# Heads' output gates, squares, roots and scaling computed inside the token mixers, one head late

## The chip, the cores and the metric

One core of a Trainium2 chip runs the whole program. The metric is the device time of one execution in microseconds; before the change it was 4261.61 us, the median of 3 runs (4261.18 to 4262.74). Engines are called by their names: TensorE (PE for its matmuls, PEld for its weight loads), VectorE (DVE), ScalarE (ACT), GpSimd (POOL) and SyncE (SP), which issues most of the transfers.

## The reference

The program is one inference step of a small trunk of two layers over 640 tokens (128 context, 512 latent), model width 1024. Layer 0 mixes tokens with HGRN2, layer 1 with GLA; both are followed by a PEER expert mixer. What matters here is the end of each token mixer:

```python
def _gated_head_norm(o, gate, w):
    of = o.astype(f32)
    y = of * lax.rsqrt(jnp.mean(of * of, axis=-1, keepdims=True) + EPS)
    return y * w.astype(f32) * jax.nn.silu(gate.astype(f32))

def _hgrn2_mixer(h, w_in, lb, gnorm_w, w_out, s_f, s_b):
    z = h @ w_in            # q, iv, f_f, f_b, og
    ...
    o = _gated_head_norm(o, og.reshape(b_, L, H_A, DV_A), gnorm_w)
    return o.reshape(b_, L, DVT_A).astype(h.dtype) @ w_out, S_f, S_b
```

HGRN2 has 8 heads of value width 128, GLA 4 heads of value width 256. The normalisation is per token and head. Its output goes through the 1024 x 1024 matrix w_out, is scaled and added to the residual stream.

## The kernel before, in words

Activations lie transposed: 128 channels on the partitions, the 640 tokens along the row (T = 640, NT = 5 tiles of 128 tokens, DC = 8 chunks of channels, NV = 1 or 2 value chunks a head). fp32 products are made of three fp32r products of high and low parts, so every weight chunk is first split: w_hi by ScalarE, w_lo by VectorE or GpSimd.

`mixer` (L502) is one stage with one instruction stream per engine, and a loop over the heads in each stream. The first H - 1 heads run in a hardware loop, the last is written out with `final=True`. The order inside a head is written by hand.

- TensorE (`head` in the tensor block): `project` for the late chunks j (values, output gates og) and the first early chunk or two of the next head; transposes of keys and values (`turn`, L1158); scores into pS (`level_scores`, L1173, and `near_scores`, L1183); the state products (L1214); the rest of the next head's early chunks; the output products (L1227).
- ScalarE: `value_chunk` or `copy` takes projections out of the two banks pp (L787); `next_hi` splits weights (L768); `keep` stores doubled products (L849); `output_gates` copies og out; at the end of a head `decays(h + 1)` does the next head's sigmoids (L825 to L835), and then the head's output goes to oT tile by tile (L933).
- VectorE: the decayed queries (L1024), seven `double` steps (L1030, L1033) with a weight split `lo` between some of them (L1012), masks (L1076 to L1084), states (L1097). In GLA also the convolutions (L993).
- GpSimd: only a weight split for the next head (L738).
- SyncE: loads weights and states and stores each head's og to the memory buffer og_spill (L708).

`mix_out` (L1242) is the next stage. It loads og of all heads back (L1280), takes sigmoids on ScalarE (L1322) and products with og on GpSimd (L1303). ScalarE and VectorE square all of oT (L1318, L1411), TensorE sums the squares with one-column matmuls (L1348), VectorE makes the mean's inverse (L1417, L1419), ScalarE its root (L1324), TensorE spreads it over the partitions (`spread`, L1355). Per chunk k VectorE multiplies by the norm weight and gate (`gated`, L1395) and by the root (`normal`, L1403), ScalarE takes the high part (L1329), VectorE the low part (L1408), and TensorE multiplies with the first two output weight chunks (L1362). The other six weight chunks follow (w_hi L1315, w_lo L1298). A stage ends with a barrier over all engines (L55).

Of the kernel before, what the change touches and what calls it, by code (L numbers as in the profile page):

```python
# [16 lines left out]
P = 128  # L17
# [79 lines left out]
def build_program(nc, a, out, upto=99):  # L97

    x_sp = nc.dram_tensor("xT_spill", [P, DC, T], F32, kind="Internal").ap()
    og_sp = nc.dram_tensor("og_spill", [DC, P, T], F32, kind="Internal").ap()  # L100
# [3 lines left out]
    with ctx:  # L104
        c = {}
        for name, shape, dt in [
            ("ident", [P, P], F32), ("ones_d", [P, P], F32), ("ones_h", [P, P], F32),
            ("coarse_mask", [P, NT, P], BF16), ("fine_mask", [P, NF, FINE], BF16), ("room", [P, 624], F32),
# [52 lines left out]
def setup(nc, a, c, x_sp, x_saved):  # L161
# [4 lines left out]
    with ExitStack() as s:  # L166
# [49 lines left out]
        def _(pool):  # L216
# [6 lines left out]
            pool.memset(c["one"][:, :], 1.0)  # L223
            pool.memset(fold[:, :], 0.0)
# [277 lines left out]
def mixer(nc, a, c, mx, h_hi, h_lo, og_sp, out, layer, x_saved):  # L502
# [7 lines left out]
    s_new = out[3 if mx.gla else 2][0, 0]  # L510
    L, E = len(mx.late), len(mx.early)
# [11 lines left out]
    with ExitStack() as s:  # L523
# [3 lines left out]
        w_raw = [sb(f"w_raw{i}", [P, DC, P]) for i in range(2)]  # L527
        w_hi = [sb(f"w_hi{i}", [P, DC, P], F32R) for i in range(2)]
        w_lo = [sb(f"w_lo{i}", [P, DC, P], F32R) for i in range(2)]
# [21 lines left out]
         o_done, o_out, s_in, s_out, og_done, og_out, q_sig_done, sp_passed, act_passed) = (  # L551
            sem(n) for n in ("w_hi_done", "lo_first", "lo_dve", "proj", "copied", "f_ready", "qk_ready", "turned",
                             "turned_out", "kv", "s_done", "att", "masked", "o_done", "o_out", "s_in", "s_out",
                             "og_done", "og_out", "q_sig_done", "sp_passed", "act_passed"))
# [8 lines left out]
        block = s.enter_context(nc.Block())  # L563

# [24 lines left out]
        def chunks_done(h, j):  # L589

            return h * NCH + (PRE + E + made(j) + 1)

# [86 lines left out]
        def _(sp):  # L679
# [12 lines left out]
            def head(h, final):  # L692
# [25 lines left out]
            sp.sem_inc(og_out, 16)  # L718
# [12 lines left out]
            sp.wait_ge(og_out, 16 * H + 16)  # L731

        @block.gpsimd
        def _(pool):
# [6 lines left out]
            def head(h, final):  # L741
                if not final:
# [14 lines left out]
            with pool.Fori(0, H - 1) as h:  # L757
                head(h, False)
# [3 lines left out]
        def _(act):  # L762
# [101 lines left out]
            def output_gates(h, n, final, which=BOTH):  # L864
                if n == 0 and 0 in which:
                    act.wait_ge(og_out, h * 16 + 16)
                copy(og[:, n, :], NV + n, h, which=which)
                if 1 in which:
                    next_hi(h, NV + n, final)

            def head(h, final):

                if mx.gla:
# [25 lines left out]
                    act.drain().then_inc(og_done, 1)  # L899
# [11 lines left out]
                else:  # L911
# [6 lines left out]
                    act.drain().then_inc(og_done, 1)  # L918
                    keep(h, 3, 5)
                    if not final:  # L920
                        early(h, 0, (0,))
                    keep(h, 5, 7)
# [8 lines left out]
                for t in range(NT):  # L931
# [3 lines left out]
                    if t == 2 and mx.gla and not final:  # L935
                        decay_exp(h + 1)

# [23 lines left out]
            with act.Fori(0, H - 1) as h:  # L961
# [4 lines left out]
        def _(dve):  # L966
# [48 lines left out]
            def head(h, final):  # L1015
# [9 lines left out]

                def double(s0, s1):
# [11 lines left out]
                if mx.gla:  # L1038
# [18 lines left out]
                else:  # L1057
# [9 lines left out]
                    lo(h, 2, final)  # L1067
                    double(1, 3)
                    lo(h, 3, final)
                    double(3, 7)  # L1070
                    lo(h, 4, final)

                dve.wait_ge(att, h + 1)
# [14 lines left out]
                for i, (d, t) in enumerate(WITH_STATE):  # L1088
# [10 lines left out]
                    dve.drain().then_inc(s_done, 1)  # L1099
# [1315 lines left out]
```

## Time and profile before

| | us |
|---|---|
| median of the runs | 4261.61 |
| the profiled execution's own time | 4259.91 |
| its span, first to last instruction | 4258.0 |
| TensorE matmuls busy | 3923.1 (92%) |
| VectorE busy | 3443.8 (81%) |
| ScalarE busy | 1704.9 (40%) |
| GpSimd busy | 1835.2 (43%) |
| mean granted TensorE clock | 0.954 |

The HGRN2 mixer and its output projection lie between about 99 and 635 us of the span, those of GLA between about 2257 and 2675 us. The rest is setup, retrieval and the expert mixers, which the diff does not touch. A timeline row reads: start, duration, engine, line, operation, output<-inputs, shape, count of merged instructions, and in brackets the idle time before it with what released it. A fp32 matmul of the plain type counts as two instructions (x2). Neighbouring matmuls overlap, so their price is the distance of their starts, not their duration.

### The profile page before, as it was taken

To read this page: it belongs to the slowest core of one execution; us is meant where nothing else is said; L and a number is where in the kernel's file an instruction comes from. 1 tells how busy PE (TensorE), PEld (TensorE's weight loads), DVE (VectorE), ACT (ScalarE), POOL (GpSimd) and SP (SyncE) were. 2 spreads that over 40 slices of the span, in tenths; PEclk is the share of its full clock that TensorE was granted. 3 is DMA by queue.
4 is the path that set the end of the run, shared out by engine and by line. 5 is a ranking of instruction groups with operands and counts; after the bars stand their busy time and mean duration, and the time that the engine had idled before them with its cause. 6 is when DMAs were issued, how large, how long until landed. Compare 5 with 4: busy or idle time off the path is not lost. (4 is left out here: it accounts for less than half of the span.)

```text
span 4258.0 us, 75035 instructions
## 1 busy us (share of the span) xinstructions
PE 3923.1 (92%) x25855; PEld 3549.5 (83%) x25855; DVE 3443.8 (81%) x6395; ACT 1704.9 (40%) x2682; POOL 1835.2 (43%) x1261
## 2 busy tenths in 40 slices
PE   6899889878999999999987888858899999999997
PEld 3899888757999999999977888856799999999997
DVE  6565547987888889999986784799788888999997
ACT  6565524354333333333335652216433333333333
POOL 2100037555445455656551003206445454556664
PEclk9999889989999999999998998979999999999999
DMA  7222135349999999999972112205999999999995
GB/s 298 65 70 60 64 107 166 116 103 288 367 362 362 363 362 358 362 362 362 363 272 59 56 48 92 72 17 135 312 362 357 367 361 364 356 362 364 360 362 219
DMA packets 620189, 1049.52 MB, mean 246 GB/s; under 512 B 229763, under 2 KB 405318, under 8 KB 619590
## 3 DMA queue, kind: packets, MB, share of 16 engines
q1 hardware_dynamic: 471520, 508.69, 35.4%
q0 software_dynamic: 147456, 536.94, 34.0%
q10 hardware_dynamic: 1126, 2.79, 0.2%
q8 instruction: 48, 0.79, 0.1%
q14 instruction: 39, 0.32, 0.0%
HBM read 982.75 MB, written 65.54 MB: 246 GB/s over the span
## 5 line engine op out<-in xcount | busy, mean ns | idle before, releaser
L2095 POOL DMA_INDIRECT rows_ex<-in_peer_v,ctx_index x512 | 707.7, 1382 | 476.7 <-DVE row_acc_ex L2174 361.0
L2095 POOL DMA_INDIRECT rows_ex<-in_peer_u,ctx_index x512 | 586.7, 1146 | 636.9 <-DVE dots_ex L2177 502.1
L2260 PE MATMUL pu_ex<-h_hi,uT_hi_ex 128*128 128x384 f32 x2048 | 715.9, 350 | 1.9 <-ACT coef_ex L2124 1.0
L2174 DVE SCALAR_TENSOR_TENSOR row_acc_ex<-rows_ex,factor_ex,row_acc_ex 128x1024 f32<-128x1024 f32 x512 | 658.0, 1285 | 52.8 <-issue 11.1
L2260 PE MATMUL pu_ex<-h_hi,uT_lo_ex 128*128 128x384 f32 x2048 | 693.0, 338 | 0.0
L2260 PE MATMUL pu_ex<-h_lo,uT_hi_ex 128*128 128x384 f32 x2048 | 693.0, 338 | 0.0
L2268 PE MATMUL py_ex<-v_hi_ex,c_hi_ex 128*128 128x512 f32 x1536 | 622.6, 405 | 0.0
L2177 DVE CUSTOM_DVE_ANT_0 rows_ex<-rows_ex,h_row_ex 128x1024 f32<-128x1024 f32 x512 | 604.6, 1218 | 0.0
L2268 PE MATMUL py_ex<-v_lo_ex,c_hi_ex 128*128 128x512 f32 x1536 | 601.3, 391 | 0.0
L2268 PE MATMUL py_ex<-v_hi_ex,c_lo_ex 128*128 128x512 f32 x1536 | 601.1, 391 | 0.0
L2113 ACT ACTIVATE uT_hi_ex<-pT_ex 128x512 fp32r<-128x512 f32 x512 | 303.6, 593 | 509.2 <-PE pT_ex L2253 490.5
L2165 DVE TENSOR_TENSOR uT_lo_ex<-pT_ex,uT_hi_ex 128x512 fp32r<-128x512 f32 x512 | 352.2, 688 | 177.3 <-ACT uT_hi_ex L2113 158.6
L2119 ACT ACTIVATE v_hi_ex<-v_raw_ex 128x1024 fp32r<-128x1024 f32 x256 | 271.7, 1062 | 486.6 <-PE py_ex L2268 486.6
L2260 PEld LDWEIGHTS pu_ex<-h_hi,uT_hi_ex 128*128 128x128 f32 x2048 | 386.0, 188 | 12.8 <-DVE uT_lo_ex L2165 1.5
L2260 PEld LDWEIGHTS pu_ex<-h_lo,uT_hi_ex 128*128 128x128 f32 x2048 | 386.5, 189 | 9.8
L2260 PEld LDWEIGHTS pu_ex<-h_hi,uT_lo_ex 128*128 128x128 f32 x2048 | 385.5, 188 | 0.0
L2268 PEld LDWEIGHTS py_ex<-v_lo_ex,c_hi_ex 128*128 128x128 f32 x1536 | 288.3, 188 | 64.0
L2268 PEld LDWEIGHTS py_ex<-v_hi_ex,c_lo_ex 128*128 128x128 f32 x1536 | 289.5, 188 | 43.2
L2268 PEld LDWEIGHTS py_ex<-v_hi_ex,c_hi_ex 128*128 128x128 f32 x1536 | 288.8, 188 | 42.6
L2188 DVE TENSOR_TENSOR v_lo_ex<-v_raw_ex,v_hi_ex 128x1024 fp32r<-128x1024 f32 x256 | 312.0, 1219 | 0.0
L2253 PE MATMUL pT_ex<-ident,u_raw_ex 128*128 128x128 f32 x2040 | 306.6, 273 | 3.0 <-DVE uT_lo_ex L2165 1.5
L2253 PEld LDWEIGHTS pT_ex<-ident,u_raw_ex 128*128 128x128 f32 x2040 | 254.0, 140 | 47.3 <-DVE uT_lo_ex L2165 3.0
(460 smaller groups left out, 7729.5 us busy)
## 6 DMA issues: line engine op xcount, KB each, us to landing
u_raw_ex<-in_peer_u SPq DMA_DIRECT2D x256, 512.0 KB
v_raw_ex<-in_peer_v SPq DMA_DIRECT2D x256, 512.0 KB
gates<-stage_ro SPq DMA_DIRECT2D x12, 4096.0 KB, 16.0
g_raw_ex<-gates SPq DMA_DIRECT2D x256, 192.0 KB
ada<-in_ada_w SPq DMA_DIRECT2D x12, 2048.0 KB, 12.1
ada_re<-in_ada_w SPq DMA_DIRECT2D x16, 1536.0 KB, 7.0
w_raw_hgrn<-in_hgrn_w_in SPq DMA_DIRECT2D x40, 512.0 KB
w_raw_re<-in_peer_w_q SPq DMA_DIRECT2D x32, 512.0 KB, 4.4
```

Of the source, the lines that this page charges most:

```text
L2095: pool.indirect_dma_start(out=rows[m % RING][:, :], out_offset=None, in_=a["peer_u" if m < TG * NC else "peer_v"].rearrange("l n d -> (l n ...
L2113: act.activation(uT_hi[b][:, 4 * part:4 * part + 4, :], pT[:, :, :], ACT.Copy) \
L2119: act.activation(v_hi[b][:, :], v_raw[b][:, :], ACT.Copy).then_inc(v_hi_done, 1)
L2165: nc.vector.tensor_sub(uT_lo[b][:, at, :], pT[:, :, :], uT_hi[b][:, at, :].bitcast(F32)) \
L2174: nc.vector.scalar_tensor_tensor(row_acc[g][:, :], rows[j][:, :], factor[:, j:j + 1], row_acc[g][:, :], ALU.mult, ALU.add).then_inc(row_fr ...
L2177: nc.vector.tensor_tensor_reduce(rows[j][:, :], rows[j][:, :], h_row[g][:, :], 1.0, 0.0, ALU.mult, ALU.add, accum_out=dots[:, j:j + 1]).th ...
L2188: nc.vector.tensor_sub(v_lo[b][:, :], v_raw[b][:, :], v_hi[b][:, :].bitcast(F32)).then_inc(v_lo_done, 1)
L2253: last_ = nc.tensor.transpose(pT[:, k, :], u_raw[b][:, (4 * part + k) * P:(4 * part + k + 1) * P], c["ident"][:, :])
L2260: last_ = nc.tensor.matmul(pu[:, 0:TD], w[:, k, :], x[:, k, 0:TD], start=(k == 0 and w is uT_hi[b] and x is h_hi), stop=(k == DC - 1 and w ...
L2268: last_ = nc.tensor.matmul(py[2 * t + i][:, :], w[:, t * P:(t + 1) * P], x[:, i * HALF_D:(i + 1) * HALF_D], start=(first and w is c_hi[b] ...
```

## The change

The og store and its loads go, with the buffer og_spill and the store's semaphores. In the mixer, per head h:

- ScalarE's `output_gates` now makes for each half of the tokens a sigmoid into `sig_og` (the room of am) beside the copy of og; GpSimd multiplies og by it (`gate_in`, `gate_done`).
- After the copies to oT, ScalarE squares the head's output (`squares`) into the room of tt.
- In head h + 1, TensorE sums the squares (`sums`) after `project(h, 0)` and spreads the root (`spread`) after `project` of j = 2; VectorE does `gate` after the first doublings, `mean_squares` after the second, `norm` after the last; ScalarE does `roots` among its `keep` steps. TensorE waits for `normed` ahead of the level scores from 3 on.
- In the last head all of this is also done for the head itself, at its end. There SyncE loads the first two output weight chunks and ScalarE and GpSimd split them.
- Head 0 is written out ahead of the loop, in each engine's stream.

`mix_out` keeps the high and low parts, the products and the residual sum. The inverse's epsilon, the room and the weight buffers move only in memory.

```diff
@@ build_program
-                mixer(nc, a, c, mx, h_hi, h_lo, og_sp, out, layer, x_saved)
-                mix_out(nc, a, c, mx, h_hi, h_lo, og_sp, x_sp, layer)
+                    mixer(nc, a, c, mx, h_hi, h_lo, weights, out, layer, x_saved)
+                    mix_out(nc, a, c, mx, h_hi, h_lo, weights, x_sp, layer)
@@ mixer
+        sig_og = am[:, :, :].rearrange("p t j -> p (t j)")
+        scratch = tt[:, :, :].rearrange("p n j -> p (n j)")
+        sq = [scratch[:, n * T:(n + 1) * T] for n in range(NV)]
+        root = c["inv"][:, 0:NT]
+        spread_at = [pO[:, t, :] for t in range(NT - 1)] + [pS[:, 8 * P:9 * P]]
@@ mixer, sync
-                sp.wait_ge(og_done, h + 1)
-                sp.dma_start(og_sp[bass.ds(h * NV, NV)].rearrange("n p t -> p n t"), og[:, :, :]).then_inc(og_out, 16)
-                if not final:
+                if final:
+                    for b in range(2):
+                        sp.wait_ge(*lo_done(h, L - 2 + b))
+                        sp.dma_start(w_raw[b][:, :, :], w_out[:, :, b * P:(b + 1) * P]).then_inc(w_loaded[b], 16)
+                else:
@@ mixer, gpsimd
             def head(h, final):
+                for n in range(NV):
+                    pool.wait_ge(gate_in, h * NV + (n + 1))
+                    pool.tensor_tensor(og[:, n, :], og[:, n, :], sig_og, ALU.mult).then_inc(gate_done, 1)
+                if final:
...
@@ mixer, scalar
             def output_gates(h, n, final, which=BOTH):
-                if n == 0 and 0 in which:
-                    act.wait_ge(og_out, h * 16 + 16)
-                copy(og[:, n, :], NV + n, h, which=which)
+                if 0 in which:
+                    if n:
+                        act.wait_ge(gate_done, h * NV + n)
+                    elif not (isinstance(h, int) and h == 0):
+                        act.wait_ge(gated, h)
+                for i in which:
+                    cols = halves()[i][1]
+                    act.wait_ge(proj, halves_done(h, NV + n, i))
+                    act.activation(sig_og[:, cols], pp[i][:, 0:HALF], ACT.Sigmoid)
+                    last = act.activation(og[:, n, cols], pp[i][:, 0:HALF], ACT.Copy)
+                    last.then_inc(copied, 1)
                 if 1 in which:
+                    act.drain().then_inc(gate_in, 1)
                     next_hi(h, NV + n, final)
+            def squares(h):
+                act.drain()
+                for n in range(NV):
+                    act.activation(sq[n], oT[:, bass.ds(h * NV + n, 1), :].rearrange("p o t -> p (o t)"), ACT.Square) \
+                        .then_inc(squared, 1)
+            def roots(h):
+                act.wait_ge(inverted, h + 1)
+                act.activation(root, root, ACT.Sqrt).then_inc(rooted, 1)
@@ mixer, scalar, head of HGRN2
                     keep(h, 3, 5)
                     if not final:
                         early(h, 0, (0,))
+                    if not first_of(h):
+                        roots(h - 1)
                     keep(h, 5, 7)
@@ mixer, scalar, end of head
+                squares(h)
+                if final:
+                    for b in range(2):
+                        act.wait_ge(w_loaded[b], w_out_loaded(b))
+                        act.wait_ge(proj, halves_done(h, L - 2 + b, 1))
+                        act.activation(w_hi[b][:, :, :], w_raw[b][:, :, :], ACT.Copy).then_inc(w_hi_done, 1)
+                    roots(h)
@@ mixer, vector
+                def gate(h):
+                    dve.wait_ge(squared, h * NV + NV)
+                    dve.wait_ge(gate_done, h * NV + NV)
...
+                    last.then_inc(gated, 1)
+                def norm(h):
+                    dve.wait_ge(o_spread, h + 1)
...
+                    last.then_inc(normed, 1)
+                def mean_squares(h):
+                    dve.wait_ge(summed, h + 1)
+                    nc.vector.tensor_scalar(root, pS[:, 0:NT], float(D / mx.dv), EPS, ALU.mult, ALU.add)
+                    dve.drain()
+                    nc.vector.reciprocal(root, root).then_inc(inverted, 1)
@@ mixer, vector, head of HGRN2
                     double(0, 1)
                     lo(h, 2, final)
+                    if not first:
+                        gate(h - 1)
                     double(1, 3)
                     lo(h, 3, final)
+                    if not first:
+                        mean_squares(h - 1)
                     double(3, 7)
+                    if not first:
+                        norm(h - 1)
                     lo(h, 4, final)
+                dve.wait_ge(gate_done, h * NV + NV)
                 dve.wait_ge(att, h + 1)
@@ mixer, tensor
+            def sums(h):
+                pe.wait_ge(squared, h * NV + NV)
...
+                last.then_inc(summed, 1)
+            def spread(h):
+                pe.wait_ge(rooted, h + 1)
...
+                last.then_inc(o_spread, 1)
             def head(h, final):
+                at_start = isinstance(h, int) and h == 0
                 for j in range(L):
                     project(h, j)
+                    if j == 0 and not at_start:
+                        pe.wait_ge(o_out, h * NT + 1)
+                        sums(h - 1)
+                    if j == 2 and not at_start:
+                        spread(h - 1)
                 if not final:
                     project(h, L)
-                    if not mx.gla:
-                        project(h, L + 1)
+                if not mx.gla and not at_start:
+                    spread(h - 1)
+                if not final and not mx.gla:
+                    project(h, L + 1)
@@ all four engines
-            with pe.Fori(0, H - 1) as h:
+            head(0, False)
+            with pe.Fori(1, H - 1) as h:
                 head(h, False)
             head(H - 1, True)
@@ mix_out
-            for k in range(0, DC, 2):
-                act.activation(sq[:, k, :], oT[:, k, :], ACT.Square).then_inc(sq_act, 1)
-            ...   # sigmoids, root, first two w_hi
             for k in range(DC):
-                act.wait_ge(y_done, k + 1)
-                act.activation(h_hi[:, k, :], y[k % 3][:, :], ACT.Copy).then_inc(hi_done, 1)
+                act.activation(h_hi[:, k, :], oT[:, k, :], ACT.Copy).then_inc(hi_done, 1)
```

## Rows read from the trace of the kernel before

**Rows 1.** Timeline of ScalarE and TensorE at the HGRN2 output projection

```profile
523.38 2.62 ACT L1318 ACTIVATE sq_mo<-x 128x640 f32<-128x640 f32 x4 [0.91 <-PEq L55]
...
524.17 15.77 PE L1348 MATMUL pp_mo<-ones_d,sq_mo 128*128 128x1 f32 x80 [2.02 <-ACT sq_mo L1318]
...
549.43 0.44 PE L1362 MATMUL pp_mo<-h_hi,w_hi_mo 128*128 128x320 f32 x1 [3.80 <-DVE h_lo L1408]
...
572.81 0.31 PE L1362 MATMUL pp_mo<-h_lo,w_hi_mo 128*128 128x320 f32 x1
...
572.96 0.31 PE L1362 MATMUL pp_mo<-h_hi,w_lo_mo 128*128 128x320 f32 x1
```

**Rows 2.** Stretches: busy us of PE, PEld, DVE, ACT, POOL; then clock, DMA, GB/s

```profile
549.40:554.00 4.60, 4.57 (x23) 4.57 (x24) 4.09 (x4) 0.74 (x1) 3.48 (x2) 0.63 0.38 114
...
2443.00:2447.00 4.00, 4.00 (x16) 4.00 (x16) 2.70 (x4) 3.79 (x6) 0.00 (x0) 0.50 0.00 0
```

**Rows 3.** All instructions of a line in the output stages; min/median/max ns

```profile
L1315 ACT ACTIVATE w_hi_mo<-w_raw_mo x16: 1038/1060/1062, 540.9 to 2647.4; 128x1024 fp32r<-128x1024 f32 x16
...
L1303 POOL TENSOR_TENSOR og_mo<-og_mo,sg_mo x16: 1528/2112/2138, 529.1 to 2594.0; 128x640 f32<-128x640 f32 x16
...
L1395 DVE SCALAR_TENSOR_TENSOR x<-x,vec,og_mo x16: 878/1620/2172, 530.8 to 2602.9; 128x640 f32<-128x640 f32 x16
...
L1403 DVE TENSOR_TENSOR y_mo<-x,spread_s_mo x16: 686/687/689, 543.5 to 2610.0; 128x512 f32<-128x512 f32 x16
...
L1403 DVE TENSOR_TENSOR y_mo<-x,spread_c_mo x16: 280/280/281, 544.1 to 2610.6; 128x128 f32<-128x128 f32 x16
...
L1329 ACT ACTIVATE h_hi<-y_mo x16: 736/738/743, 544.5 to 2610.9; 128x640 fp32r<-128x640 f32 x16
...
L1408 DVE TENSOR_TENSOR h_lo<-y_mo,h_hi x16: 824/826/2954, 546.4 to 2611.7; 128x640 fp32r<-128x640 f32 x16
```

**Rows 4.** Timeline of TensorE, a spread at full clock

```profile
555.72 1.05 PE L1355 MATMUL spread_s_mo<-ident,inv 128*128 128x128 f32 x8
...
556.75 0.39 PE L1362 MATMUL pp_mo<-h_hi,w_hi_mo 128*128 128x320 f32 x1
```

**Rows 5.** Timeline and stretch of HGRN2 loop heads

```profile
241.74 0.41 PE L497 MATMUL pp_hgrn<-h_hi,w_hi_hgrn 128*128 128x320 f32 x1
...
247.80 0.47 ACT L933 ACTIVATE x<-pS_hgrn 128x128 f32 x2
...
261.62 0.42 ACT L787 ACTIVATE g_hgrn<-pp_hgrn 128x320 f32<-128x320 f32 x1
...
288.69 0.41 PE L497 MATMUL pp_hgrn<-h_hi,w_hi_hgrn 128*128 128x320 f32 x1
...
188.00:235.00 47.00, 45.87 (x580) 45.03 (x579) 28.43 (x44) 28.23 (x46) 2.35 (x1) 1.00 0.23 68
```

**Rows 6.** Timeline of ScalarE, a table load in the HGRN2 mixer

```profile
140.31 1.28 ACT L825 ACT_TABLE_LOAD   x1
...
141.60 1.27 ACT L825 ACTIVATE run_hgrn<-g_hgrn 128x1280 f32<-128x1280 f32 x1
```

**Rows 7.** Timeline of TensorE in the last HGRN2 head

```profile
499.07 1.08 PE L1158 MATMUL pT_hgrn<-ident,run_hgrn 128*128 128x128 f32 x4 [8.30 <-DVE run_hgrn L1033]
...
510.45 1.05 PE L1214 MATMUL pO_hgrn<-tt_hgrn 128*128 128x128 f32 x7 [1.05 <-issue]
```

**Rows 8.** Timeline of three engines in a GLA head

```profile
2442.64 0.63 PE L497 MATMUL pp_gla<-h_hi,w_hi_gla 128*128 128x320 f32 x1 [4.27 <-ACT zc_gla L796]
...
2459.66 1.47 ACT L849 ACTIVATE ex_gla<-run_gla 128x640 f32<-128x640 f32 x2
...
2462.43 1.22 DVE L1012 TENSOR_TENSOR w_lo_gla<-w_raw_gla,w_hi_gla 128x1024 fp32r<-128x1024 f32 x1 [0.31 <-ACT w_hi_gla L768]
```

**Rows 9.** Timeline of TensorE at the GLA output projection

```profile
2592.70 0.63 PE L1362 MATMUL pp_mo<-h_hi,w_hi_mo 128*128 128x320 f32 x1 [4.43 <-DVE h_lo L1408]
...
2614.25 0.31 PE L1362 MATMUL pp_mo<-h_hi,w_lo_mo 128*128 128x320 f32 x1
```

More of the change, by code:

```diff
@@ L499, in split_product, with mixer @@
     return last
-def mixer(nc, a, c, mx, h_hi, h_lo, og_sp, out, layer, x_saved):
+def mixer(nc, a, c, mx, h_hi, h_lo, weights, out, layer, x_saved):
     oT = c["x"]
@@ L510, in mixer @@
     s_new = out[3 if mx.gla else 2][0, 0]
+    w_out = a["gla_w_out" if mx.gla else "hgrn_w_out"][0].rearrange("(k p) n -> p k n", p=P)
+    gw = VEC["gla_g" if mx.gla else "hgrn_g"]
+    w_raw, w_hi, w_lo = weights
     L, E = len(mx.late), len(mx.early)
@@ L921, in head @@
                         early(h, 0, (0,))
+                    if not first_of(h):
+                        roots(h - 1)
                     keep(h, 5, 7)
@@ L960, in _ @@
                 decay_exp(0)
-            with act.Fori(0, H - 1) as h:
+            head(0, False)
+            with act.Fori(1, H - 1) as h:
                 head(h, False)
@@ L1067, in head @@
                     lo(h, 2, final)
+                    if not first:
+                        gate(h - 1)
                     double(1, 3)
                     lo(h, 3, final)
+                    if not first:
+                        mean_squares(h - 1)
                     double(3, 7)
+                    if not first:
+                        norm(h - 1)
                     lo(h, 4, final)
+                dve.wait_ge(gate_done, h * NV + NV)
                 dve.wait_ge(att, h + 1)
@@ L1099, in head @@
                     dve.drain().then_inc(s_done, 1)
+                if final:
+                    gate(h)
+                    mean_squares(h)
+                    norm(h)
+                    dve.drain()
                 if ODD and not final:
@@ L1115, in _ @@
                 conv(0, 0, 1)
-            with dve.Fori(0, H - 1) as h:
+            head(0, False)
+            with dve.Fori(1, H - 1) as h:
                 head(h, False)
@@ L1200, in head @@
                         level_scores(t, l)
+                if not at_start:
+                    pe.wait_ge(normed, h)
                 for l in range(3, NL):
@@ L1229, in head @@
                     last.then_inc(o_done, 1)
+                if final:
+                    pe.wait_ge(o_out, h * NT + NT + 1)
+                    sums(h)
+                    spread(h)
             nm.tensor(pe)
@@ L1236, in _, with mix_out @@
             project_early(-1, L + 1)
-            with pe.Fori(0, H - 1) as h:
+            head(0, False)
+            with pe.Fori(1, H - 1) as h:
                 head(h, False)
             head(H - 1, True)
-def mix_out(nc, a, c, mx, h_hi, h_lo, og_sp, x_sp, layer):
-    NV, H = mx.nv, mx.heads
+def mix_out(nc, a, c, mx, h_hi, h_lo, weights, x_sp, layer):
     AHEAD = 2
     w_out = a["gla_w_out" if mx.gla else "hgrn_w_out"][0].rearrange("(k p) n -> p k n", p=P)
-    gw = VEC["gla_g" if mx.gla else "hgrn_g"]
+    w_raw, w_hi, w_lo = weights
     oT = c["x"]
@@ L1274, in _ @@
         @block.sync
         def _(sp):
-            def weights(j):
+            for j in range(AHEAD, DC):
+                if j >= 2 * AHEAD:
+                    sp.wait_ge(w_lo_done, j - 2 * AHEAD + 1)
                 sp.dma_start(w_raw[j % AHEAD][:, :, :], w_out[:, :, j * P:(j + 1) * P]).then_inc(w_loaded[j % AHEAD], 16)
-            def gates(i):
-                sp.dma_start(og[:, 2 * i:2 * i + 2, :], og_sp[2 * i:2 * i + 2].rearrange("k p t -> p k t")) \
-                    .then_inc(og_in[i], 16)
@@ L1342, in _ @@
         def _(pe):
-            def sums(g):
-                for k in range(g * NV, (g + 1) * NV):
-                    pe.wait_ge((sq_act, sq_dve)[k % 2], k // 2 + 1)
-                for t in range(NT):
-                    for k in range(g * NV, (g + 1) * NV):
-                        last = nc.tensor.matmul(rows[:, g * NT + t:g * NT + t + 1], sq[:, k, t * P:(t + 1) * P],
-                                                c["ones_d"][:, 0:1], start=(k % NV == 0), stop=(k % NV == NV - 1))
-                last.then_inc(summed, 1)
-            def spread(g):
-                for t in range(NT):
-                    dst = spread_s[g % 2][:, t, :] if t < NT - 1 else spread_c[g % 2][:, :]
-                    last = nc.tensor.matmul(dst, inv[:, g * NT + t:g * NT + t + 1].to_broadcast([P, P]),
-                                            c["ident"][:, :], start=True, stop=True)
-                last.then_inc(spread_done, 1)
             def terms(j, k, i, cols):
@@ L1365, in terms @@
                 return last
-            for g in range(H):
-                sums(g)
-            pe.wait_ge(rooted, 1)
-            spread(0)
-            spread(1)
             for k in range(DC):
```

147 lines of the change are left out of this document (54 added, 93 removed).

## The prediction

> **What bounds the kernel now.** I read the page's slices first: TensorE is busy in nearly every slice, but two narrow places are neither full nor at full clock, the ends of the two token mixers. Then the timeline of each engine over the end of the HGRN2 mixer and the output projection behind it. There the reader is to see [rows 1]: the stage begins at 523.38 us, after a 0.91 us hand-over between stages; TensorE spends 15.77 us on 80 one-column matmuls for the heads' sums of squares; the first output product starts at 549.43, 26.05 us into the stage, and the eight first groups of products (j = 0 and 1 together) end at 573.1. In the GLA layer the same first product is at 2592.70, and the groups end at 2614.4 [rows 9]. That front is serial and is what the change takes apart. Third, one head inside each mixer, engine by engine. An HGRN2 head lasts 46.95 us (241.74 to 288.69) [rows 5], six times over, and TensorE is the bound in it: 45.87 of 47 us busy. In a GLA head TensorE waits 4.27 us for ScalarE's copy of a projection, while VectorE goes from its doublings to the weights' low part and on into the convolution without a gap over 0.31 us [rows 8]; the VectorE chain is the bound. So work moved into HGRN2 heads is paid on TensorE, and work moved into GLA heads on VectorE.
>
> **What goes: the front of the two output projections.** HGRN2. Behind the last head's output copies (about 0.9 us before 523.38, so 522.5) there now stands: squares 0.73 us plus a drain 0.1; ten one-column matmuls at 15.77/80 = 0.197 us each [rows 1], 2.0, to 525.3. Beside them ScalarE makes the two weight copies (1.06 + 0.95, [rows 3]) and loads the square root's table, 1.28 [rows 6], so its root is not ready before 526.8. The spread of ten matmuls takes 1.03 us at full clock (555.72 to 556.75, [rows 4]), so 2.1 at half, and 0.3 until its result is used: 529.2. Normalising is 0.69 + 0.28 [rows 3]: 530.2; hand-over 0.9: 531.1. Then a high part 0.74 and a low part 0.82 [rows 3], and the first product starts at 532.7 instead of 549.43: 16.7 us gained. The products were paced by spreads between them; now they are 96 matmuls at 0.147 (572.81 to 572.96, [rows 1]) = 14.1, plus 2.0 for a start at half clock like that of 549.4 to 554 [rows 2], 16.1 instead of 23.6: 7.4 gained. Together 24.1. What follows, the wait for the third weight chunk's low part, stays. GLA by the same steps, with two squares (1.44), twenty sums (3.9), a spread (2.4) and four pieces of normalising (1.9): the stage begins 10.4 us later than now, the first product at 2579.2 instead of 2592.70, 13.5 gained, and 16.1 instead of 21.7 for the products, 5.6: together 19.1. **Sum of gains 43.2.** The gates' trip through memory, their loads and the 16 sigmoids and products of the stage go with this front and count no second time.
>
> **What comes, HGRN2 heads 1 to 6.** (a) *Square roots need another table.* A table load takes 1.28 us [rows 6] and there is none in the loop now, since it holds only sigmoids and copies. With a root in the middle of the head there are two: one ahead of the root, one back ahead of the next decays' sigmoid, where ScalarE has just come free and TensorE is about to start the next head. ScalarE ends its output copies at 248.27, 6.5 us into the head [rows 5]; now 7.8, then drain and square, 8.65. TensorE ends the head's first product at 7.04 (48 matmuls) and waits for the squares in order to sum them: 1.6. (b) The sums. A one-column matmul at full clock is not in the trace; bounds are 0.103 (a 128-column one of the same type, ten in 1.03, [rows 4]) and 0.197 (at the lower clock, [rows 1]). I take 0.11, it is the weight load that they share: 1.1 us. (c) The spread: 1.1. (d) The wait for the root. TensorE comes to the spread 7.04 x 3 + 2.7 = 23.8 us into the head. ScalarE's copy of the second early half, behind which the root stands, starts at 19.9 (261.62, [rows 5]); before it now come the reload 1.28, the square 0.8, two half-width sigmoids 0.7 (a copy of that shape is 0.42, [rows 5], 0.35 net), and a wait of 1.4 for VectorE's gate product (0.80 net each, [rows 3]), which also makes the doublings later; then the table 1.28 and the root 0.21. That would be 25.8; some 0.8 of it lies in waits that ScalarE has in the head now, so 25.0: 1.2 us of waiting. (e) *GpSimd beside VectorE.* The gate product on GpSimd takes 1.53 to 2.14 us; VectorE's two-input products took 0.88 to 2.17 and 0.82 to 2.95 us in the same stage, the long ones where GpSimd ran [rows 3]. In the mixer GpSimd runs now only where VectorE is idle. The new product falls amid the doublings. Bounds are 0 and 2.1 us a head; I take 1.3, the excess of the middle ones, and it lengthens (d) to 2.5. Per head 1.6 + 1.1 + 1.1 + 2.5 = 6.3, six heads: 37.8. Head 0 has only (e): 0.9. Head 7 has no early projections; TensorE waits 8.3 us for VectorE there [rows 7], so ScalarE's and VectorE's additions count: 1.28 + 0.8 + 0.8 (gate) + 0.45 (mean, inverse, drain), and half of (e): 4.0. **HGRN2 heads +42.7.**
> The Trainium skill, SBUF — State Buffer, section "Who interferes with whom", says that a VectorE instruction with two inputs in SBUF and a GpSimd instruction that reads SBUF exclude each other for a whole instruction. By it each GpSimd gate product costs VectorE up to its own 1.53 us, and the products with an input in PSUM, the normalising, are free of it. By that rule (e) is 1.5 in place of 1.3, and the sum 2 us higher; the trace agrees in kind, with its 2.17 and 2.95 us.
> The Trainium skill, ScalarE: Activation LUTs, section "What ACT_TABLE_LOAD costs", gives 2.66 us for a switch with its drain. The row disagrees: the load starts at 140.31 and the next sigmoid at 141.60 [rows 6], 1.29. By the page's figure a head with two loads would grow by 2.8 more.
>
> **What comes, GLA.** The squares and sums lie in the 4.27 us that TensorE waits now. VectorE's chain takes everything else: two gate products 1.6, mean and inverse 0.45, normalising 1.6. Ahead of the normalising it must wait for the spread: ScalarE ends its last level copies at 2461.1 [rows 8], +2.05 for VectorE's additions, +0.4 sigmoid, table 1.28, root 0.2, spread 1.1: 2466.1, while VectorE is ready at 2462.4 + 2.05 = 2464.5. So 3.65 + 1.6 + latencies = 5.5 per head, for heads 1 to 3, 0.9 for head 0 (squares, sigmoids): 17.4. GpSimd's second product falls in the value convolution, which has no gap: 1.3 x 4 = 5.2. **GLA heads +22.6.**
>
> **The rest.** Head 0 stands ahead of the loop as code of its own. Engines arriving at new code lost 1.05 us once at 510.45 [rows 7]; I take 1.5 per mixer, 3.0, with 0 and 6 as bounds. The last head's two weight loads are issued by SyncE as soon as a buffer is free, in place of the next head's; covered by over 30 us. The gates' stores were 8 + 4 issues that nobody waited for: nothing.
>
> **Sum:** 42.7 + 22.6 + 3.0 - 43.2 = +25.1. The profiled execution took 4259.9 us, with a span of 4258.0; that gives 4285. The median of the runs is 4261.6, 1.7 above the profiled one, so 4287; I say 4286.
>
> **Rivals.** *A, all but TensorE's instructions is hidden* (4234): the reloads and waits fall into slack that I do not see. HGRN2 then pays 7 x 2.2 = 15.4 and GLA nothing: -43.2 + 15.4 = -27.8, with the profiled 4259.9 and the 1.7 above it. For it: ScalarE and VectorE are each busy 28 of 47 us in a head [rows 5]. Against: the output copies end only 0.5 us ahead of TensorE's need [rows 5], so a reload of 1.28 cannot be hidden. It decides from a ScalarE that reaches the root before 23.8 and the squares before 7.0. *B, GpSimd and VectorE do not disturb each other* (4272): 9.4 less in HGRN2 and 5.2 less in GLA: +10.5. For it: the slow products may owe something to transfers. Against: GpSimd's own time grew as well. *C, the new waits drop the clock* (4301): TensorE waited 4.27 us at 2442.6 and ran at half clock until 2447 [rows 2, 8], some 2 us lost. Waits of 2.5 us in nine heads would cost 9 x 1.6 = 14.4 more: +40. The 1.1 us waits of now do not drop it.
>
> **Chances.** My forecast 0.42, B 0.20, C 0.16, A 0.22. What can be told from no change is 0.2%, 8.5 us. My forecast and C are slower (0.58), B mostly (0.13 of 0.20, the rest same), A mostly faster (0.17 of 0.22, 0.05 same). So faster 0.17, same 0.12, slower 0.71. The likeliest case by itself spans 4276 to 4296; for 8 in 10 the range goes to 4240 below, short of A's full gain, and 4305 above, past C.
>
> **What would show it.** Two table loads in each HGRN2 loop head and a period of 53 us instead of 46.95 (49 under A, 51.9 under B); TensorE waiting about 1.6 us for squares and 2.5 for the root; VectorE's doubling products of over 0.82 us beside GpSimd's gate; a GLA head 5.5 to 7 us longer; the first output product some 10 us after the hand-over's old place in HGRN2, and the clock row at 1.0 through the HGRN2 loop (C: not). I am wrong if the HGRN2 loop grows by less than 3 us a head, or if the front of the output stages gives back more than 50.

## The result

| | median us | runs | profiled run, span |
|---|---|---|---|
| before | 4262.03 | 4 (4261.18 to 4262.74) | 4259.91, 4258.0 |
| after | 4286.23 | 4 (4282.37 to 4289.79) | 4282.37, 4280.5 |

The ratio is 1.0055, 95% interval 1.0043 to 1.0068: slower by 24 us. The forecast was 4286, slower. The profiled run of after is the fastest of its four; the working below is made against its span, +22.5 us.

Where they went is read by noting, in both traces, the start of the same instruction: the sigmoid of the queries in each HGRN2 head, the first output copy in each GLA head (it stands at the head's end), the first and last product of the output stages. The differences of the positions add up to the span, but for rounding. The "groups" are the first eight groups of products in an output stage.

| part | forecast | measured |
|---|---|---|
| HGRN2 heads, to the last output matmul (head 0's new code, 1.5, with it) | +44.2 | +49.6 |
| HGRN2 front and first eight groups of products | -24.1 | -25.6 |
| the rest of HGRN2's output stage | 0 | -1.5 |
| from its last product to GLA's first (not touched) | 0 | -4.3 |
| GLA head 0, to its first output copy (new code, 1.5, with it) | +3.7 | 0.0 |
| GLA heads 1 to 3 | +20.4 | +24.7 |
| GLA front and groups | -19.1 | -19.6 |
| from there to the end | 0 | -0.7 |
| sum | +25.1 | +22.5 |

By head, HGRN2 grew by 2.4, 7.9, 8.4, 5.6, 6.9, 5.6, 6.9 and 5.8 us (forecast 2.4, six times 6.3, 4.0), and starts 0.2 later; GLA by 0, 8.8, 8.0 and 7.9 (forecast 3.7, then 6.8 each).

### The profile page after: what moved, and what is told of

Its sections match the earlier page's. It is cut to its first block and busy times, and to the rows that moved or that the text cites. A ratio compares the mean times of both kernels' runs of the same rounds, so it can differ in the third digit from the quotient of the medians.

```text
span 4280.5 us, 74914 instructions
## 1 busy us (share of the span) xinstructions
PE 3920.4 (92%) x25855; PEld 3546.2 (83%) x25855; DVE 3425.5 (80%) x6407; ACT 1733.4 (40%) x2734; POOL 1832.6 (43%) x1262
```

## The profile after

The end of HGRN2, timeline of ScalarE, TensorE and VectorE, answers to [rows 1, 3, 4, 7]:

```profile
571.94 0.74 ACT L914 ACTIVATE tt_hgrn<-x 128x640 f32<-128x640 f32 x1
572.58 1.99 ACT L998 ACTIVATE w_hi<-w_raw 128x1024 fp32r<-128x1024 f32 x2
574.57 0.21 ACT L920 ACTIVATE inv<-inv 128x5 f32<-128x5 f32 x1
...
543.98 2.07 PE L1270 MATMUL pO_hgrn<-ident,inv 128*128 128x128 f32 x8 [6.22 <-ACT inv L920]
...
571.15 0.39 PE L1365 MATMUL pS_hgrn<-am_hgrn,tt_hgrn 128*128 128x128 f32 x2
...
572.82 1.25 PE L1263 MATMUL pS_hgrn<-ones_d,tt_hgrn 128*128 128x1 f32 x10 [1.28 <-ACT tt_hgrn L914]
574.83 2.07 PE L1270 MATMUL pO_hgrn<-ident,inv 128*128 128x128 f32 x8 [0.77 <-ACT inv L920]
...
581.56 0.63 PE L1444 MATMUL pp_mo<-h_hi,w_hi 128*128 128x320 f32 x1 [4.23 <-DVE h_lo L1468]
...
596.95 0.31 PE L1444 MATMUL pp_mo<-h_hi,w_lo 128*128 128x320 f32 x1
600.03 0.41 PE L1444 MATMUL pp_mo<-h_hi,w_hi 128*128 128x320 f32 x1 [2.77 <-POOL w_lo L1417]
...
577.48 0.69 DVE L1108 TENSOR_TENSOR x<-x,pO_hgrn 128x512 f32<-128x512 f32 x1 [2.94 <-PE pS_hgrn L1270]
```

The 15.77 us of 80 one-column matmuls for the sums are gone; ten take 1.25. The last output matmul starts at 571.15 (521.52 before) and the first output product at 581.56: 10.4 us behind it, where it was 27.9. There is no table load ahead of this root (the forecast had counted one, 1.28): the last head has no next decays, so the table of the root before is still there. The first product waits for the activations' low part, not for the weights.

A loop head, the same engines, answers to [rows 5, 6]:

```profile
305.11 1.28 ACT L855 ACT_TABLE_LOAD   x1
...
321.24 0.44 ACT L903 ACTIVATE am_hgrn<-pp_hgrn 128x320 f32<-128x320 f32 x1 [1.48 <-DVE x L1097]
...
328.63 1.47 ACT L879 ACTIVATE ex_hgrn<-run_hgrn 128x640 f32<-128x640 f32 x2 [1.66 <-DVE run_hgrn L1127]
...
330.45 1.28 ACT L920 ACT_TABLE_LOAD   x1
331.75 0.21 ACT L920 ACTIVATE inv<-inv 128x5 f32<-128x5 f32 x1
...
315.20 1.25 PE L1263 MATMUL pS_hgrn<-ones_d,tt_hgrn 128*128 128x1 f32 x10 [1.49 <-ACT tt_hgrn L914]
...
332.01 1.16 PE L1270 MATMUL pO_hgrn<-ident,inv 128*128 128x128 f32 x8 [1.37 <-ACT inv L920]
...
325.75 1.66 DVE L1076 TENSOR_TENSOR w_lo<-w_raw,w_hi 128x1024 fp32r<-128x1024 f32 x1 [0.87 <-ACT w_hi L798]
...
324.54 1.79 POOL L764 TENSOR_TENSOR og_hgrn<-og_hgrn,am_hgrn 128x640 f32<-128x640 f32 x1 [32.78 <-ACTq L907]
```

Both waits that the forecast named are there: 1.49 us for the squares (1.6 forecast) and 1.37 for the root (2.5 forecast). ScalarE comes to both late. One load stands directly ahead of the root, the other ahead of the decays at 305.11, with the work that leads to the squares (314.32) close behind it. The load ahead of the root stands behind 1.66 us in which ScalarE waited for VectorE. The last two rows belong to term (e): VectorE's weight split begins while GpSimd's gate product still runs, and takes 1.66 us.

The stretches from head to head, heads 2 to 6, then parts of heads 4 and 7 (columns as in [rows 2]; the column ahead of the last two is the granted clock as a share of full speed):

```profile
253.35:308.74 55.39, 51.65 (x600) 50.33 (x599) 30.54 (x48) 32.00 (x54) 3.94 (x2) 0.94 0.18 52
308.74:361.25 52.51, 48.52 (x599) 47.20 (x599) 30.65 (x48) 32.09 (x53) 4.15 (x2) 1.00 0.19 55
361.25:415.05 53.80, 50.06 (x599) 48.74 (x599) 30.43 (x48) 32.10 (x54) 3.94 (x2) 0.97 0.18 53
415.05:467.56 52.51, 48.54 (x599) 47.22 (x599) 30.65 (x48) 32.07 (x54) 4.15 (x2) 1.00 0.19 55
467.56:521.37 53.81, 50.06 (x599) 48.81 (x599) 30.46 (x48) 32.10 (x53) 3.95 (x2) 0.97 0.18 54
...
369.30:372.70 3.40, 3.40 (x16) 3.40 (x15) 2.66 (x3) 2.77 (x4) 0.00 (x0) 0.54 0.00 0
540.00:553.70 13.70, 8.02 (x59) 6.79 (x61) 7.56 (x13) 8.00 (x14) 0.21 (x1) 0.51 0.00 0
```

Heads 4 and 6 are 1.3 us longer than heads 3 and 5, and in each lie 3.4 us at half clock (0.54 in a window that is cut a little wide), shortly behind the wait for the squares. In head 2 it is 6.8 us, and the head is 2.9 longer. Before, the clock was 1.00 in these heads. The longest such stretch, 13.7 us, begins within the 6.22 us wait of the last head.

Head 1 is 2.4 us longer than head 3 for another reason. It is the loop's first pass, and TensorE waits in it for nothing that the profile shows:

```profile
237.63 0.74 PE L1319 MATMUL pS_hgrn<-ex_hgrn 128*32 128x32 f32 x64 [1.88 <-issue]
```

In head 0, which is code of its own now, such waits at the same line are 1.03 and 2.72 us. Before, they were 0.90 and 2.17, all in head 0, which then was the loop's first pass.

GLA, TensorE, VectorE and ScalarE, answers to [rows 8, 9]:

```profile
2387.91 0.64 PE L500 MATMUL pp_gla<-h_hi,w_hi 128*128 128x320 f32 x1 [1.62 <-ACT zc_gla L826]
...
2491.72 1.65 PE L1270 MATMUL pO_gla<-ident,inv 128*128 128x128 f32 x6 [4.50 <-ACT inv L920]
...
2494.37 0.69 DVE L1108 TENSOR_TENSOR x<-x,pO_gla 128x512 f32 x1 [3.26 <-PE pS_gla L1270]
...
2490.16 1.28 ACT L920 ACT_TABLE_LOAD   x1
...
2491.68 1.28 ACT L903 ACT_TABLE_LOAD   x1
...
2621.57 0.63 PE L1444 MATMUL pp_mo<-h_hi,w_hi 128*128 128x320 f32 x1 [4.58 <-DVE h_lo L1468]
```

The old wait of TensorE, 4.27 us, is 1.62 in this head (0.94 and 0.71 in the two behind it); the sums lie in it. The new one is VectorE's for the spread, 2.63, 3.26 and 3.27 us in heads 1 to 3. The spread waits 4.5 us for the root, and ahead of the root stands its table.

## The experiments

Each time is given as the difference to runs of before on the same chip; after stands at +24.2 by its own.

**Taking away the table.** no_switch_2:

```
-  act.activation(root, root, ACT.Sqrt).then_inc(rooted, 1)
+  act.activation(root, root, ACT.Copy).then_inc(rooted, 1)
```

> After, with a Copy in place of each mixer's square root, so that ScalarE loads no other table inside a mixer; leaves out the root of the heads' mean squares. My theory (table loads of 1.28 us cause most of the wait for the squares and half of that for the root): HGRN2 heads 1 to 6 lose 2.7 us each (16), head 7 about 2, the root's table and the one back in three GLA heads 1.3 to 2.5 each (6): about -24, so 4262 against 4286. Rival A (the reloads lie in slack; what costs is only TensorE's own work): 0 to -5, 4281 to 4286.

4255.48 against 4263.15, ratio 0.9983 (0.9974 to 0.9993): -7.7, so 31.9 less than after. HGRN2's heads 2 to 6 take 49.81 us each, all at clock 1.00. Timeline of TensorE, one head:

```profile
353.75 1.25 PE L1263 MATMUL pS_hgrn<-ones_d,tt_hgrn 128*128 128x1 f32 x10 [0.20 <-ACT tt_hgrn L914]
...
369.12 1.16 PE L1270 MATMUL pO_hgrn<-ident,inv 128*128 128x128 f32 x8
```

Both waits are gone, 1.49 to 0.20 and 1.37 to none: 2.7 us a head as expected. With them goes the half-clock time of heads 2, 4 and 6, 5.5 us together, which my number of -24 left out. Rival A is refuted: the loads are the largest single cause. Without them the change is a small gain.

**One part of the additions at a time, on the kernel before.** before_switches adds the loads alone, before_pe_work TensorE's matmuls alone (the first added line is HGRN2's of before_switches, the rest is before_pe_work):

```
+act.activation(c["inv"][:, 0:NT], c["one"][:, 0:1].to_broadcast([P, NT]), ACT.Sqrt)
...
+def extra():
+    for t in range(NT):
+        dst = pO[:, t, :] if t < NT - 1 else pS[:, 8 * P:9 * P]
+        nc.tensor.matmul(dst, c["ones_d"][:, 0:1].to_broadcast([P, P]), c["ident"][:, :],
+                         start=True, stop=True)
...
     project(h, j)
+    if j == 0:
+        pe.wait_ge(o_out, h * NT + 1)
+        for t in range(NT):
+            for n in range(NV):
+                nc.tensor.matmul(pS[:, t:t + 1], c["ident"][:, :], c["ones_d"][:, 0:1],
+                                 start=(n == 0), stop=(n == NV - 1))
+    if j == 2:
+        extra()
...
+if not mx.gla:
+    extra()
```

> Before, with one square root of five columns in each mixer head at the place where the change puts its root, its result unused (in GLA a sigmoid of five columns behind it, so that the table comes back at once): the table loads alone. My theory: nothing on TensorE waits for the squares or the root here, so what is left is the reload ahead of the next decays in HGRN2, which puts ScalarE's output copies 1.3 us later, about 0.8 behind TensorE's need in six or seven heads: +5 in HGRN2; GLA +2.8 x 3 at most where ScalarE's last level copies bound VectorE, nearer +3: 4270. Rival A (slack takes them): 4262.

> Before, with the change's matmuls on TensorE alone: the sums (5 or 10 products of one column for each 128 columns) behind each head's first projection and the five spread products further on, from constant data, waiting for nothing of ScalarE or VectorE; in all eight heads of HGRN2 and all four of GLA. My theory: 1.1 + 1.1 us in each HGRN2 head, +17.6 (TensorE is the bound); in GLA the sums lie in the wait of 4.3 us and the spread's 1.1 to 1.5 in VectorE's shadow: 0; 4280. Rivals: the same under A and B; if the one-column products run at the weight load of 0.2 us, +3.1 a head, 4287.

before_switches: 4279.86 against 4261.91, 1.0042 (1.0025 to 1.0059), +18.0, more than twice the +8 expected. before_pe_work: 4285.07, 1.0050 (1.0034 to 1.0067), +23.2. Stretches of one loop head each, the first of before_switches:

```profile
345.38:393.65 48.27, 46.15 (x580) 44.97 (x579) 28.42 (x43) 30.59 (x51) 2.36 (x1) 1.00 0.22 67
```

and of before_pe_work:

```profile
346.20:395.39 49.19, 48.05 (x599) 47.23 (x598) 28.35 (x43) 28.46 (x48) 2.36 (x1) 1.00 0.22 65
```

From 46.95 the loads alone make 48.27, +1.32 in every loop head behind head 0 (which grew by 3.5, not explained): TensorE waits 0.99 us for the value copy behind ScalarE's reload, though nothing asks for a root. They made GLA's heads 3.1 and 3.9 us longer in two of three, where VectorE waits up to 3.3 us for the third weight's high part (0.3 before). TensorE's matmuls make 49.18 to 49.19, +2.24 against 2.2 expected. From the first sum (204.76) to the next product (205.79) ten one-column matmuls at full clock take 1.03 us, 0.103 each. GLA's heads 1 and 2 stay at 72.75: nothing, as expected. The profiled run is the slowest of the four, its span 28.8 us above that of before: 16.2 lie in HGRN2's heads before the last, 2.5 in the last, 3.9 from there to GLA's first matmul, in code that is the same in both kernels, 2.0 in GLA's head 0, and 4.2 behind it.

**GpSimd's product.** small_pool_2:

```
-  pool.tensor_tensor(og[:, n, :], og[:, n, :], sig_og, ALU.mult)
+  pool.tensor_tensor(og[:, n, 0:1], og[:, n, 0:1], sig_og[:, 0:1], ALU.mult)
```

> After, with GpSimd's gate product cut to one column of 640; leaves out the gate of the other columns. My theory (GpSimd's product holds VectorE back 1.3 us in each HGRN2 head and lengthens the wait for the root by as much): -1.3 x 7 = -9 in HGRN2, about -1 x 3 in GLA, 4274. Rival B (the two don't disturb each other): 4286.

4280.68 against 4263.15, 1.0042 (1.0025 to 1.0059): +17.5, 6.7 less than after; the interval is too wide to tell the two from each other by the median. The trace tells: a loop head is 52.08 in place of 52.51 and the wait for the root 0.91 in place of 1.37. So 0.43 us a head, a third of the 1.3 that I took, and not the 0 of rival B. It equals what the weight split beside the product loses, 1.66 us in after, 1.23 here:

```profile
326.70 1.23 DVE L1076 TENSOR_TENSOR w_lo<-w_raw,w_hi 128x1024 fp32r<-128x1024 f32 x1 [0.86 <-ACT w_hi L798]
```

GLA's heads 1 to 3 together are only 0.3 us shorter, against 3 expected and 5.2 for four heads in the prediction.

**The sums later.** late_sums_2:

```
-  if j == 0 and not at_start:
+  if j == 1 and not at_start:
       pe.wait_ge(o_out, h * NT + 1)
       sums(h - 1)
```

> After, with the sums of squares issued by TensorE behind the head's second projection in place of the first. My theory: the wait of 1.5 us for the squares goes in six HGRN2 heads, -9, unless the mean, which VectorE takes in 20 us into the head, comes later by it: 4277. In GLA it stands in a place where TensorE waited anyhow: 0, or + where the second projection's copy no longer covers the 2.4 us of 20 sums. Rival: TensorE's idle time only moves behind the sums, to the root that it waits for: 4286.

4280.0 against 4261.91, 1.0040 (1.0025 to 1.0054): +18.1. Every loop head from the third on takes 52.50, waits of TensorE from 253 to 516 us:

```profile
PE pp_hgrn L500 <- ACT v_hgrn L817: 8.5, 5, 1.7
PE pO_hgrn L1270 <- ACT inv L920: 5.5, 5, 1.1
```

The wait for the squares (1.5) became one of 1.7 for the copy that ScalarE makes next. The rival was right that it moves, but not that it moves to the root. ScalarE is late as a whole, by the reload; whatever TensorE asks of it first shows the wait. The 6 us won are mostly those of heads 2, 4 and 6: none drops its clock now, with waits of 1.7 and 1.1 in each. So a wait's length alone does not tell whether the clock falls.

**The weights late.** weights_late_2 loads and splits the first two weights in the output stage again; the loops of SyncE, GpSimd and ScalarE there start at chunk 0, of which GpSimd's:

```
-  for j in range(AHEAD, DC):
+  for j in range(DC):
-      pool.wait_ge(w_hi_done, j - AHEAD + 1)
+      pool.wait_ge(w_hi_done, j + 1)
```

> After, with the first two output weights loaded and split in the output stage again, as before the change; all else as after. My theory: the stage's first product then waits for the load (3 us), two high parts (2 x 1.0) and the low part on GpSimd (2.2), 7 us from the start of the stage, where the activations' first low part now lets it go at about 2.7: +4 to +5 a layer, 4295. Rival (the activations' split ends last anyway, the weights hide beside it): 0 to +1, 4286.

4296.55, 1.0086 (1.0069 to 1.0103), +34.6, 10.4 more than after. The first HGRN2 product, timeline of TensorE:

```profile
570.94 2.08 PE L1256 MATMUL pO_hgrn<-ident,inv 128*128 128x128 f32 x8 [0.77 <-ACT inv L910]
...
583.72 0.60 PE L1436 MATMUL pp_mo<-h_hi,w_hi 128*128 128x320 f32 x1 [10.27 <-POOL w_lo L1404]
```

It is 12.78 us behind the spread, in after 6.73: 6.05 in HGRN2 and 5.7 in GLA, against 4 to 5 expected. That part of the change does what it is for. Its HGRN2 loop heads do the same work as those of after and have the same waits, 1.5 us for the squares and up to 1.4 for the root; yet heads 2, 3, 4 and 6 take 53.8 us at clock 0.97 and head 5 alone 52.5 at 1.00. Head 3, which had full clock in after:

```profile
305.93:359.73 53.80, 50.05 (x599) 48.73 (x599) 30.45 (x48) 32.11 (x53) 3.95 (x2) 0.97 0.18 54
```

**The loads where ScalarE is idle.** The first two hunks behind the helper are HGRN2's, the last is GLA's, where VectorE's mean and inverse also move up behind its second doubling: tables_ahead, and, with the product held back and the sums later, tables_ahead_quiet ("the kernel before in this list" is tables_ahead):

```
+def table(func):
+    act.activation(c["inv"][:, NT:NT + 1], c["one"][:, 0:1], func)
...
-keep(h, 3, 5)
+keep(h, 3, 4)
+if not first_of(h):
+    table(ACT.Sqrt)
+keep(h, 4, 5)
...
+table(ACT.Sigmoid)
 early(h, 2)
 decays(h + 1)
...
 keep(h, 2, 4)
+if not first_of(h):
+    roots(h - 1)
+    table(ACT.Sigmoid)
 value_chunk(h, 1, (1,))
```

> After, with the same work but the table loads moved to where ScalarE is idle. HGRN2: one square root of one column ahead of the last level copy but two (ScalarE waits 1.7 us for VectorE behind it), and one sigmoid of one column ahead of the copies of the early projections (3.1 us idle). GLA: mean and inverse on VectorE behind its second doubling, root and a one-column sigmoid in ScalarE's 2.8 us of idle time behind the fourth level copy. My theory (what costs is not the loads but that TensorE waits for what stands behind them): HGRN2 heads come to 49.8 to 50.4 us as with no switch at all, from 53.2: -20; GLA heads lose TensorE's wait for the root of 4.5 us and VectorE's of 2.6: -4 x 3; about 4254, below before. Rival (a load costs ScalarE 1.28 us wherever it stands, and ScalarE or VectorE bounds the head): HGRN2 heads 51 or more, 4270 and above.

> As the kernel before in this list, and in HGRN2 the sums behind the second projection, and GpSimd's gate product held back until VectorE has made its last doubling, where VectorE waits for TensorE. My theory: GpSimd's product cost 0.43 us a head by the cut to one column, the sums' place nothing once the squares are early: 7 x 0.4 = -3, 4251. Rival (held back, the product makes the gates late for ScalarE's next projection or the mask, and TensorE waits): slower than the kernel before by 5 or more.

4261.35 against 4262.58, 0.9999 (0.9989 to 1.0008): -1.2; and 4259.82, 0.9992 (0.9982 to 1.0002): -2.8. HGRN2 did what was expected: 49.81 us for each of heads 2 to 6 with both loads in it, the same as with none.

```profile
349.45:399.26 49.81, 48.48 (x599) 47.23 (x598) 30.60 (x48) 32.48 (x55) 4.14 (x2) 1.00 0.20 58
```

Holding the product back gave nothing (49.87). GLA failed: 80.97 and 80.48 us, as in after. TensorE's wait for the root is gone, but timeline of ScalarE and VectorE in tables_ahead:

```profile
2458.14 1.47 ACT L879 ACTIVATE ex_gla<-run_gla 128x640 f32<-128x640 f32 x2 [3.50 <-DVE run_gla L1136]
2459.63 1.28 ACT L924 ACT_TABLE_LOAD   x1
...
2464.37 1.23 DVE L1085 TENSOR_TENSOR w_lo<-w_raw,w_hi 128x1024 fp32r<-128x1024 f32 x1 [3.72 <-ACT w_hi L798]
```

I had put the root behind the copy that ends ScalarE's idle time, not ahead of it. The 3.5 us idle pass unused, and the loads then stand ahead of a weight copy that VectorE needs.

**Three lines up, and the normalising late.** root_between moves the root ahead of that copy, against tables_ahead (the first diff); norm_late moves root, spread and normalising to the second half of the GLA head (the second, TensorE's part):

```
-keep(h, 2, 4)
+keep(h, 2, 3)
 if not first_of(h):
     roots(h - 1)
     table(ACT.Sigmoid)
+keep(h, 3, 4)
```

```
+if mx.gla and not at_start:
+    pe.wait_ge(s_done, h * 8 + 8)
+    spread(h - 1)
 if not final:
     project_early(h, L + 1 if mx.gla else L + 2)
 pe.wait_ge(masked, h + 2)
+if mx.gla and not at_start:
+    pe.wait_ge(normed, h)
```

> As tables_ahead, but in GLA the root and the one-column sigmoid stand ahead of the fourth level copy in place of behind it. The trace of tables_ahead shows ScalarE idle for 3.5 us ahead of that copy and VectorE then waiting 3.7 us (0.7 before) for the third weight's high part, behind the two loads. My theory: the loads (2.8 us) go into the 3.5 us, VectorE's wait falls back to 0.7, GLA heads from 80.6 to 77.5: -9, so about 4252. Rival (a load taken anywhere in a GLA head costs the head as much; it is ScalarE's work that counts): 80.6, 4261.

> As tables_ahead, but in GLA root, spread and normalising stand where the engines wait: the root behind the copies of the turned values (ScalarE 9.4 us idle), the spread ahead of the early projections, the normalising behind the state updates (VectorE idle for 6.5 us); the gates' product stays amid the doublings. My theory: all that is left on VectorE's chain is the gates' product 1.6, mean and inverse 0.4, and what GpSimd's product holds up, 1.1: GLA heads 72.76 + 3.1 = 75.9 against 80.6, three of them: -14; less the spread's 1.1 us now on TensorE ahead of the projections that VectorE's next convolution waits for: +3. About 4250. Rival (the spread and the wait for the normalising put the outputs late, 1.9 to 3 us a head more): 4256.

root_between: 4254.37 (11 runs) against 4261.77 (21 runs), ratio 0.9982 (0.9973 to 0.9991): -7.4. VectorE's wait in it:

```profile
2458.35 1.23 DVE L1086 TENSOR_TENSOR w_lo<-w_raw,w_hi 128x1024 fp32r<-128x1024 f32 x1 [0.69 <-ACT w_hi L798]
```

3.72 fell back to 0.69, the heads to 78.4, 78.5 and 61.2 (77.5 expected for a loop head). This version, with the same arithmetic as after, beats both kernels. norm_late: 4262.37, 1.0002 (0.9993 to 1.0011), +0.6, worse than both my 4250 and its rival's 4256; the loop heads of GLA take 79.6 and 81.1 where I expected 75.9. Stretch from the state updates to the outputs, in norm_late:

```profile
2489.80:2515.90 26.10, 23.95 (x113) 20.32 (x114) 15.86 (x27) 10.41 (x14) 2.91 (x2) 0.77 0.03 10
```

and in tables_ahead:

```profile
2490.00:2516.00 26.00, 21.98 (x139) 18.78 (x140) 17.23 (x27) 12.39 (x19) 4.82 (x2) 1.00 0.03 11
```

The mean clock is 0.77 in place of 1.00, and ScalarE waits 11.24 us for the early projection where it was 9.40: the spread and TensorE's wait for the last state update stand ahead of the projections that the next head begins with. How much of the loss is the clock and how much the order was not told apart.

## Why the prediction was right, step by step

No step of the forecast has the wrong sign, but several terms have the wrong size, and their errors nearly cancel.

- **Loads and waits, (a) and (d).** Right in place. At full clock a loop head grew by 5.56: 2.24 TensorE's matmuls, 1.49 the squares, 1.37 the root, 0.46 left over. The forecast's 6.3 was 2.2, 1.6 and 2.5. (The terms listed for the root's time add up to 25.6, not 25.8; little hangs on it.)
- **(b), (c).** 1.1 + 1.1 forecast, 2.24 measured by itself.
- **(e) is the term that was mis-sized.** 0.43 a head in HGRN2 in place of 1.3. Only the end of GpSimd's product falls on a two-input VectorE instruction; the rest falls where VectorE is idle or between its products. In GLA 5.2 was forecast, and cutting the product gave 0.3 in three heads. The full effect is seen in GLA's value convolution, here in head 2 of tables_ahead, where a VectorE product of 127 columns takes 1.43 us (1.67 and 1.48 in heads 1 and 3) and its neighbour of that shape 0.34:

```profile
2477.76 1.59 POOL L764 TENSOR_TENSOR og_gla<-og_gla,am_gla 128x640 f32<-128x640 f32 x1 [5.50 <-ACTq L907]
...
2478.07 1.43 DVE L1064 SCALAR_TENSOR_TENSOR v_gla<-zc_gla,vec,v_gla 128x127 f32<-128x127 f32 x1 [0.17 <-issue]
```

  It ends 0.15 behind GpSimd. The Trainium skill, SBUF — State Buffer, section "Who interferes with whom", says that a VectorE instruction with two inputs in SBUF contends with a GpSimd instruction that reads SBUF, and that the port pair they share is an exclusive lock. The trace agrees: the normalising, which has one input in PSUM, takes its usual 0.69 us at 2494.37 of after, while a gate product of 1.56 us runs from 2493.85. By that rule the price is at most what is left of the other's instruction when one arrives, under 1.8 us here and mostly far less.
- **Rival C was given too little.** It is part of the answer. Six heads at 6.3 are 37.8, measured 41.2. At full clock and behind the first pass they would have been 33.4; half-clock time added 2.9 in head 2 and 1.3 each in heads 4 and 6, 5.5 together.
- **New code.** 1.5 in each mixer's head 0 was forecast. In HGRN2 most of it came in head 1, the loop's first pass, 2.4 us longer than a later head at full clock. In GLA head 0 did not grow, 0.0 against 3.7 with the other terms.
- **Head 7.** 4.0 forecast, 5.8 measured. The root stands on the path there with TensorE waiting 6.22 us for it. Half clock was not in the sum; the head had it before too (mean clock 0.78 over 44.0 us, now 0.76 over 49.8, so about 19 and 24 us at half), and the 4 to 5 us more are worth at most half of that.
- **Fronts.** 24.1 and 19.1 forecast, 25.6 and 19.6 measured.
- **GLA heads 1 to 3.** 20.4 forecast, 24.7 measured, though the 1.3 a head of (e) is nearly absent: 8.2 a head where 5.5 was the rest of the sum. The wait ahead of the normalising was forecast as 1.6 us (2466.1 less 2464.5), and is 2.63 to 3.27. That leaves about 1 us a head open. The loads alone on the kernel before cost 3.1 and 3.9 us in heads that grew by 8.8 and 8.0.
- **The table's price.** The Trainium skill, ScalarE: Activation LUTs, section "What ACT_TABLE_LOAD costs", gives 2.66 us with its drain. Here the load starts at 305.11 and the sigmoid at 306.40, 1.29 again; the trace disagrees. Two loads of 1.28 cost a loop head 2.70 us at full clock (52.51 to 49.81), about their full length, since TensorE waited behind both; in before_switches, where nothing asked for the root, they cost 1.32.
- **The stages between.** -5.8 us, not in the sum: 1.5 in the rest of HGRN2's output stage and 4.3 from its last product to GLA's first. The latter stretch is in no diff. It is 1620.6 us before and 1616.4 after, and in the twelve profiled executions of this document it lies between 1616.2 and 1622.9, the latter in before_pe_work. Single executions differ by that much there; why is open. The median of the runs (+24.2) is nearer to the sum of 25.1 than the profiled one.

So that 24 us came out where 25 was said is partly luck. Against the profiled run, (e) and what else made the six HGRN2 heads too long by 4.4, GLA's head 0 (3.7), the stages between (5.8), the fronts (2.0) and the end (0.7) were forecast too high, 16.6 together; half clock in the HGRN2 loop (5.5), its first pass (2.4), head 7 (1.8), GLA's other heads (4.3) and the later start (0.2) too low, 14.2. The sign and its mechanism, the loads that make ScalarE late, were right and are shown: without them (and the root itself) the same change is 7.7 us faster than before, and with all of them at idle places 7.4 faster.

## What to carry to other kernels

A table load cost here what waited behind it, from nothing to its full length. Issue it with a one-column dummy where the engine is idle, and check on the trace on which side of the awaited instruction the idle time lies: in GLA three lines decided between 1.2 and 7.4 us below the kernel before. When taking a wait away, ask what the same engine delivers next; if the engine is late as a whole, the wait only changes its name.

## What was not expected of the hardware

TensorE's clock fell to half in heads 2, 4 and 6 of after, for 6.8, 3.4 and 3.4 us. Each of them has a wait of 1.5 us ahead of ten one-column matmuls. It did not fall in heads 3 and 5 with the same work and waits. In weights_late_2 it fell in heads 2, 3, 4 and 6 of the same code, in small_pool_2 in heads 2 and 4. It fell in no loop head of late_sums_2, with a wait of 1.7 us ahead of a projection and 1.1 ahead of the spread, nor in those of before_switches, where TensorE waited 0.99. Each fall of 3.4 us added 1.3 us to a head of 52.5. What decides between two like heads is open.
